# Two feed-forward tiles per half moved from plain products to the seven-product scheme, in a two-layer encoder step

## What is computed

```python
def _swiglu(x, w_gate, w_up, w_down):
    return (jax.nn.silu(x @ w_gate) * (x @ w_up)) @ w_down
# in _layer, twice:
h = h + 0.5 * _rmsnorm(_swiglu(_rmsnorm(h, g[0]), f1g, f1u, f1d), g[1])
```

## Time and profile before

| | |
|---|---|
| runs | 2678.25, 2678.82, 2679.03 us; median 2678.82 us |
| profiled execution | 2683.69 us by its own clock, of which 2681.9 us are the span of the trace |
| granted TensorE clock, mean | 0.992 of 2.4 GHz |
| instructions in the trace | 56799 |
| matmuls | 17818 |

### The profile page before, as it was taken

One profiled execution on the slowest core, in us unless ns is written; L12 is line 12 of the kernel. 1 busy time (PEld: TensorE's weight loads), 2 busy tenths in 40 slices (PEclk: granted clock), 3 DMA queues, 4 the chain that ended last, 5 costly groups with the idle time before them and its releaser, 6 DMA issues.

```text
span 2681.9 us, 56799 instructions
## 1 busy us (share of the span) xinstructions
PE 2631.2 (98%) x17818; PEld 2590.4 (97%) x17818; DVE 1721.9 (64%) x2619; ACT 1083.6 (40%) x1953; POOL 908.1 (34%) x731
## 2 busy tenths in 40 slices
PE   8999999999999999999999999999999999999998
PEld 7999999989999999999999999998999999999997
DVE  6888823575444788882388885265644448888625
ACT  5444513333333544451354444142333335454413
POOL 4665302240001566530256651142200025666112
PEclk9999999999999999999999999999999999999999
DMA  4223223222222222322223232232122222322222
GB/s 122 80 78 93 76 85 83 69 65 69 72 79 67 77 79 78 91 77 85 79 71 89 78 88 85 72 90 72 50 76 78 76 76 59 91 78 86 87 72 93
DMA packets 435462, 212.91 MB, mean 79 GB/s; under 512 B 45016, under 2 KB 433594, under 8 KB 435258
## 3 DMA queue, kind: packets, MB, share of 16 engines
q1 hardware_dynamic: 431652, 207.27, 26.9%
q10 hardware_dynamic: 3638, 3.51, 0.4%
HBM read 207.21 MB, written 5.29 MB: 79 GB/s over the span
## 4 chain that ended last, share of the span: by engine, by line
PE 92%; DVE 4%; issue 2%; ACT 1%; DVEq 0%; POOL 0%; DMA 0%; ACTq 0%; SPq 0%; POOLq 0%
PE ps L741 11%; PE ps L742 11%; PE ps L743 11%; PE ps L649 9%; PE ps L651 9%; PE ps L650 9%; PE ps L832 7%; PE ps L833 7%; PE ps L834 7%; PE ps L677 5%; PE ps L729 4%; DVE h L1685 1%; DVE x_r L1667 1%; PE ps L880 1%; PE ps L902 1%
## 5 line engine op out<-in xcount | busy, mean ns | idle before, releaser
L2315 POOL TENSOR_TENSOR w_lo<-raw,w_hi 128x512 fp32r<-128x512 f32 x288 | 429.0, 1500 | 357.8 <-ACT w_hi L1102 356.1
L741 PE MATMUL ps<-x_r,w_hi 128*128 128x320 f32 x1728 | 534.6, 309 | 3.1 <-ACT u L1102 2.8
L743 PE MATMUL ps<-x_r,w_lo 128*128 128x320 f32 x1728 | 533.9, 309 | 0.0
L1649 DVE TENSOR_TENSOR w_lo<-raw,w_hi 128x1024 fp32r<-128x1024 f32 (+1 forms) x240 | 297.6, 1243 | 355.5 <-ACT w_hi L1110 355.3
L2266 POOL TENSOR_TENSOR acc_y<-acc_y,sq 128x320 f32<-128x320 f32 x96 | 94.4, 984 | 1105.7 <-ACT sq L1120 1104.0
L742 PE MATMUL ps<-x_r,w_hi 128*128 128x320 f32 x1440 | 444.9, 309 | 0.0
L1110 ACT ACTIVATE w_hi<-raw 128x1024 fp32r<-128x1024 f32 (+1 forms) x248 | 253.5, 1027 | 468.0 <-PE ps L834 301.2
L832 PE MATMUL ps<-mid_hi,w_hi 128*128 128x320 f32 x1408 | 437.6, 311 | 0.0
L833 PE MATMUL ps<-mid_lo,w_hi 128*128 128x320 f32 x1408 | 436.1, 310 | 0.0
L834 PE MATMUL ps<-mid_hi,w_lo 128*128 128x320 f32 x1408 | 436.0, 310 | 0.0
L649 PE MATMUL ps<-x_r,w_hi 128*128 128x320 f32 x1088 | 346.8, 319 | 4.3 <-DVE w_lo L1649 4.3
(11 more groups left out here) (216 smaller groups left out, 5069.2 us busy)
## 6 DMA issues: line engine op xcount, KB each, us to landing
raw<-in_ffn_w_gate_dram SPq DMA_DIRECT2D x360, 128.0 KB, 2.3
raw<-in_ffn_w_up_dram SPq DMA_DIRECT2D x360, 128.0 KB, 2.3
raw<-in_ffn_w_down_dram SPq DMA_DIRECT2D x348, 128.0 KB, 2.2
raw<-in_w_in_dram SPq DMA_DIRECT2D x304, 128.0 KB, 2.3
raw<-in_w_branch_dram SPq DMA_DIRECT2D x64, 128.0 KB, 2.6
raw<-in_w_out_dram SPq DMA_DIRECT2D x64, 128.0 KB, 2.2
raw<-in_ffn_w_down_dram SPq DMA_DIRECT2D x68, 64.0 KB, 1.9
rows<-in_x_prompt_dram SPq DMA_DIRECT2D x4, 512.0 KB, 5.4
```

The lines of the kernel that those rows point to most:

```text
L741: pe.matmul(bank(b), wh, lhs(0, k), start=begin and k == 0, stop=False, skip_group_check=True)
L743: mm = pe.matmul(bank(b), wl, lhs(0, k), start=False, stop=k == QK - 1, skip_group_check=True)
L1649: dve.tensor_tensor(w_cols(1, hi_slot, 0, nk), raw_cols(raw_slot, 0, nk), f32(w_cols(0, hi_slot, 0, nk)), ALU.subtract).then_inc(w_split, 1)
L2315: pool.tensor_tensor(w_cols(1, slot, k0, k0 + QK), src, f32(w_cols(0, slot, k0, k0 + QK)), ALU.subtract).then_inc(ws_lo, 1)
```

## The change

`PLAIN` goes from 4 to 2: `extra_four` and all that serves it (its four loads, high and low parts, eight scalings) go away, `first_four` stays, and each FFN has 20 units instead of 18. The hand-written lists of ACT and DVE for the head are reordered; POOL's list and PE's order inside the units stay as they are, but P1 of unit 0 now stands right behind `first_four`. The four silus that remain come after `next_high(0, 0)` on ACT, and their four `head_mid` products stand together ahead of DVE's loop. S4 (`sum4`) and the low parts of S3 change places on DVE.

```diff
-PLAIN = 4
+PLAIN = 2
-HEAD_T, HEAD_LOADS, RESTAGED = 4, 2, 2
+HEAD_T, HEAD_LOADS, RESTAGED = 4, 1, 2
...
@@ SP
-                for s in range(HEAD_T):
-                    load(s, columns(w_ffn[n][s % 2], l, 0, KD, (2 + s // 2) * P, s), (w_split, w0 + s + 1))
                 for u in range(2):
-                    unit(u, PLAIN // 2, [(w_split, w0 + HEAD_T + 2 * u + 1), (w_split, w0 + HEAD_T + 2 * u + 2)])
+                    unit(u, PLAIN // 2, [(w_split, w0 + 2 * u + 1), (w_split, w0 + 2 * u + 2)])
...
@@ PE
+                pe.wait_ge(evac, g + 4 + 5)
                 p1(0, 0)
-                pe.wait_ge(evac, g + 4 + 12)
+                pe.wait_ge(inv_x_made, 2 * (3 * l + 2 * n) + 2)
                 p2(0, 0)
...
                 first_four(hi0(l, n), split0(l, n), g, seam, Y_SQUARES_MIX if n else Y_SQUARES)
-                extra_four(split0(l, n), g, seam)
                 strassen(n, l, g)
...
@@ ACT
                 roots(BX[1], sm - 1, 3, False)
-                extra_high(0)
-                head_silu(0, 0)
-                extra_high(1)
+                w0_high(0, HEAD_LOADS, (group_done, g + 5))
                 keep_inv_x(1, sm - 1)
-                extra_high(2)
-                head_silu(1, 0)
-                extra_high(3)
-                for i in range(8):
+                for i in range(4):
                     sum_hi(i)
-                head_silu(0, 1)
-                head_silu(1, 1)
-                w0_high(0, HEAD_LOADS, (group_done, g + 10))
-                head_silu(2, 0)
-                head_silu(2, 1)
-                t_high(0, "T2", 0, (group_done, g + 12))
-                t_high(0, "T1", 0, (group_done, g + 12))
+                t_high(0, "T2", 0, (group_done, g + 6))
+                t_high(0, "T1", 0, (group_done, g + 6))
+                for i in range(4, 8):
+                    sum_hi(i)
+                t_high(0, "T3", 0, (group_done, g + 7))
+                t_high(0, "T4", 0, (group_done, g + 7))
+                snap(1, 0, 0)
                 for k in range(QK):
-                    sum_hi(2 * QK + k)
-                t_high(0, "T3", 0, (group_done, g + 14))
-                t_high(0, "T4", 0, (group_done, g + 14))
-                head_silu(3, 0)
-                head_silu(3, 1)
+                    s3_high(k)
                 b22_high(0, HEAD_LOADS, (group_done, g + PLAIN_G))
                 b22_high(1, HEAD_LOADS, None)
-                for k in range(QK):
-                    s3_high(k)
-                snap(1, 0, 0)
                 w0_high(1, HEAD_LOADS, (prod, p0 + 2))
                 snap(2, 0, 0)
                 snap(3, 0, 0)
+                for k in range(QK):
+                    sum_hi(2 * QK + k)
                 next_high(0, 0)
+                for hf in range(2):
+                    for f in range(PLAIN):
+                        head_silu(f, hf)
                 silu(gate_scaled, gs0 + 1, PLAIN, 0)
                 end_unit(0, 0, 0, 1)
...
@@ DVE
                 inverse(sm - 1, 3)
-                extra_low(0)
-                for k in range(QK):
+                for k in range(2):
                     sums12(k)
+                t_first(0, 0, HEAD_LOADS)
+                for k in range(2, QK):
+                    sums12(k)
+                w0_low(0, 0)
+                t_second(0, 0)
                 second_half(sm - 1)
                 scale_first(1)
-                extra_low(1)
-                scale_extra(0)
-                extra_low(2)
-                w0_low(0, 0)
-                t_first(0, 0, HEAD_LOADS)
-                scale_extra(1)
-                t_second(0, 0)
-                extra_low(3)
+                for k in range(QK):
+                    s3_low(k)
                 for k in range(QK):
                     sum4(k)
-                scale_extra(2)
-                scale_extra(3)
-                for k in range(QK):
-                    s3_low(k)
                 w0_low(1, 1)
...
                 dve.wait_ge(silu_done, sl0 + HEAD_MIDS)
                 dve.wait_ge(evac, g + 4 + PLAIN_G)
                 alone(dve)
+                for j in range(HEAD_MIDS):
+                    head_mid(j)
                 with dve.Fori(0, UNITS // 2 - 1) as i:
-                    head_mid(i)
                     body(1, i * 2 + 1, i)
```

More of the change, by code:

```diff
@@ L205, in trunk_kernel @@
         FIRST_BANKS = ((0, 1, 2, 3), (0, 4, 6, 7))
-        EXTRA_BANKS = (1, 2, 3, 5, 4, 6, 7, 1)
         BANK_A, BANK_D, BANK_E = (0, 1), (2, 3), 5
@@ L714, in first_four @@
                 low_of_x(1)
[L716 to L731, removed]
             def product(what, u, lhs, b, begin, ready=None):
@@ L1178, in free @@
                     return (group_done, v) if kind == "group" else (chunk_done, ch0 + v)
-                def extra_high(s):
-                    stage(raw_full(s, l, n, 1), s, KD, (group_done, g + 4 + s + 1), s)
                 def head_silu(f, hf):
-                    act.wait_ge(evac, g + (4 * hf + 2 * f if f < 2 else 8 + 4 * (f - 2) + hf) + 5)
+                    act.wait_ge(evac, g + 4 * hf + 2 * f + 5)
                     act.activation(tile(mid, f, hf), tile(mid, f, hf), ACT.Silu).then_inc(silu_done, 1)
@@ L1725, in scale_first @@
                         scale((plain_gate, plain_up)[s % 2](2 * (s // 2) + hf), FIRST_BANKS[hf][s], hf, g + 4 * hf + s)
[L1727 to L1732, removed]
                 def head_mid(j):
@@ L1888, in ffn @@
                 last_quarters(0, 0, 0)
-                assert HEAD_MIDS == UNITS // 2 - 1
                 dve.wait_ge(silu_done, sl0 + HEAD_MIDS)
```

## The result

The changed kernel takes **2729.99 us** (median of 4 runs, 2729.23 to 2732.1), the kernel before 2678.53 us beside it (4 runs, 2676.95 to 2679.03): ratio 1.0195 (1.018 to 1.021), 51.5 us more; 2733 us were forecast. The profiled execution took 2730.72 us with a span of 2728.9 us, 47.0 us more than the span before. That of before lay 4.9 us above its median, that of after only 0.7 us; in what follows the traces account for 47.0 us, 11.75 per FFN. The other 4.5 us may be the clock, which isn't shown: the profiled execution of before has a mean granted clock of 0.992, as has one more execution of that kernel (2683.62 us), and eight others (2676.34 to 2678.96 us) have 0.993 to 0.995. The two traces themselves differ in this too: after the wait of the earlier trace rows the clock is lower in all four FFNs of the trace of before, and in two of that of after.

What follows compares the result with a forecast made beforehand. PE, busy 98% of the span, was taken to bound the kernel. Per FFN 6.8 + 1.8 + 5.3 + 1.8 + 1.3 - 3.5 = 13.5 us more, times four 54 us on 2678.8: 2733 us, range 2705 to 2758.

Steps and rivals of the forecast that it cites:

- What goes away: On PE, 24 fewer matmuls per FFN at 0.147 us save 3.5 us; DMAs were put at nothing.
- P1 of unit 0: After `first_four`, PE waits 6.8 us for DVE's first scaling of half 1; bounds 4.3 and 8.7.
- P1 of unit 1: PE waits 5.3 us for DVE's `w0_low`, behind S3's low parts and `sum4`; bounds none to 6.9.
- the eight DVE instructions: S3's low parts and `sum4` all meet POOL: five at 1.55, three at 1.0, 10.8 us together.
- P6 of units 0 and 1: PE waits 1.8 us before each, for POOL's low part of T2 and for ACT's `snap` 1 of unit 1.
- The clock: Lower granted clock after a wait costs PE 1.3 us; one such loss per head (0 to 5.2).
- POOL costs DVE little: Rival: in the new order they miss each other; waits of 7 us per head, 2692 to 2705 us; chance 0.08.
- The clock falls at every wait: Rival: all four waits of a head cost 1.3 us, 3.9 more per head, 2749 us; chance 0.13.
- DVE becomes the bound after the head: Rival: units 1 to 3 wait for `c22_out` 1 to 3 us more, 2737 to 2745 us; chance 0.09.
- Faster: Rival: unit 0's preparation still fits under `first_four`; without any wait 2664.7 us; chance 0.04.
- The rule on DVE beside POOL: Whole-instruction lock makes a pair 1.78 us, 3 us more per head, 2745 us; prediction stayed with the rows' 1.55.
- The rule on the clock: Skill page's kernel fell to the lower clock at each wait because its matmuls between waits were short.

Runs made afterwards that it cites:

- x1: Changed kernel plus 192 idle matmuls between `first_four` and P1 of unit 0, new list order kept; 2797.34 us, ratio 1.0442.
- x6: Changed kernel plus 192 idle matmuls after `first_four`, with ACT's and DVE's lists back in the old order; 2781.7 us, ratio 1.0383.
- x4: Changed kernel plus idle matmuls inside the two waits, 42 before P1 of unit 0 and 26 before P1 of unit 1; 2728.94 us, ratio 1.0187.
- x3: Changed kernel with POOL writing zeros for the low parts of S1, S2, S4 and unit 0's five weight parts; 2707.13 us, ratio 1.0106.
- x2: Changed kernel with `w0_low` and the first scaling on DVE after one k's sums, other sums behind the weight differences; 2732.38 us, ratio 1.02.
- x5: Changed kernel plus 96 idle matmuls between `first_four` and P1 of unit 0; 2745.51 us, ratio 1.0248.
- x8: Changed kernel with `w0_low` of unit 1 moved ahead of the four `sum4` in DVE's list; 2730.89 us, ratio 1.0194.
- x7: Kernel before, with DVE's sum for P3 in the last unit moved ahead of a staging step and six low parts; 2669.98 us, ratio 0.9967.

## Why the prediction was right, and where its terms were not

The total was 3 us off (2733 against 2729.99, in a range of 2705 to 2758), for the reason given: the preparation of unit 0 lost its cover. By spans it foresaw 54 us and 47.0 came; that the medians agree better is luck, since the profiled execution of before lay further above its median than that of after. Its steps:

- **What goes away.** 96 matmuls, as counted, with a price per matmul that x1 and x6 bear out (192 idle ones fill 28.2 us per FFN). No wait for a load turned up.
- **P1 of unit 0: right.** 6.8 us were predicted and 27.0/4 = 6.8 measured. Inside, two errors cancel in part: both first weight differences ran alone, 0.68 each, not one at 1.29; the four sums beside POOL took 4.3, not 4.0, and the first scaling came at 62.55 + 0.42, 0.7 earlier than worked out. PE started 0.3 behind it, and `first_four` was through 0.2 before the 56.9 of the prediction, which makes up for most of that: the place and the releaser were reasoned, the equal tenths are luck.
- **P1 of unit 1: right in place and releaser, too large.** 5.3 predicted, 17.2/4 = 4.3 measured. The failed term is the eight DVE instructions: 8.7 us in place of 10.8, against which S3 came 0.9 us later than worked out (67.87 for 67.0). Their price beside POOL was right (1.5 for 1.55 beside a weight part, 1.1 for 1.0 beside a low part of S4); but the prediction let all eight meet POOL, and three of them met it hardly or not at all.
- **P6 of units 0 and 1: not there in after.** Two times 1.8 us were predicted. T2's low part came at about 68.2 (69.0 predicted), while PE came to P6 only at 68.70, because the lower clock had stretched P1 and P2. For P6 of unit 1 `snap` was done at 87.2 (88.5 predicted), and PE came there at 88.2 (86.7 predicted). The step that failed is that both terms were worked out with PE at full clock. x4, with PE at full clock, shows both waits, 1.7 and 1.1, released as predicted by POOL's `w_lo` and by `snap`.
- **The clock: too small.** One loss of 1.3 us per head was taken. In the first head PE made 15 matmuls in 67.38 - 63.29 = 4.09 us where 15 x 0.147 = 2.2 would do, and 22 in 5.96 where 3.2 would do: 1.9 + 2.7 = 4.6 us. So after each wait the clock's loss took the place of the wait before P6, where the prediction added the two. That 4.6 lies so near to the 1.8 + 1.8 + 1.3 = 4.9 that were put down for both is luck: x4 shows waits of 2.8 there, not of 3.6.
- **Sum of the first head:** 6.8 + 4.3 + 4.6 - 3.5 = 12.2 us. The other three heads lose less to the lower clock, 3.9, 4.1 and 3.5 us; with the mean of 4.0 the terms make 11.6, with 11.75 per FFN in the spans. The agreement is partly luck: the lower clock in the last unit, 1.3 us in the earlier trace rows, is missing after the change in two FFNs of four, some 0.65 per FFN less, and about 0.8 per FFN is left that no row here accounts for.

**The rivals.** *POOL costs DVE little* is refuted by DVE's rows (1.03 to 1.17 for 0.54), and x3 shows what it would have been worth: 2707 us, near the 2692 to 2705 given for it. *The clock falls at every wait* holds in the trace for both waits that were there, but its price does not: x4 removes the falls and saves 1 us, not the 16 that PE's lost time in the four heads comes to. *DVE becomes the bound after the head* did not happen, and the last stretch above agree on an unbroken PE. *Faster* was excluded by 6.8 us before P1 alone; x2 took that wait away by another order of DVE's list, and it stood one product further.

**The rule on DVE beside POOL.** Four DVE instructions for S3 and S4 and four weight parts of POOL, alone 0.48 (x3) and 1.30, took 1.5 us a pair, and a sum and a low part, alone 0.54 and 0.86, took 1.09. The Trainium skill, page "SBUF — State Buffer", section "SBUF: two separate sides", with its lock for a whole instruction would make 1.78 and 1.40 of them. The trace doesn't agree with that part of the rule: the two engines went nearly one after the other, with some 0.3 us of each pair side by side. The same section limits the conflict of a DVE instruction with two SBUF inputs to POOL's instructions that read SBUF, and there the trace agrees: in x3 the sum takes 0.55 beside a fill.

**The rule on the clock.** After 6.62 and after 4.30 us without work the granted clock was 0.50, with 60 matmuls between the two waits. The Trainium skill, page "TensorE: Matmul & The Clock Gate", section "HAM oscillation — how this bites in real kernels", describes this pattern, and the trace agrees; its advice to keep PE warm brought nothing here (x4), since PE wasn't what the head waited for.

What stays open: why x5 gives 1.1 us per FFN less back than the matmuls that it leaves out. It isn't the heads: from P1 of unit 0 to the 301st matmul of the units x1 and x5 take the same 49.4 to 49.9 us, head by head. The mean clock of x5 is 0.990 against 0.994 in x1, and no run shows whether that is the cause.

## What to carry to other kernels

Work that looks redundant on the bounding engine can be the cover under which the others prepare its next stage: before taking it away, add up, list by list, when the first operand of that stage would be there, with the durations that the engines have *beside each other*. If the sum says several us, reordering may only move the wait from one product to the next (x2, x8), and keeping the clock up need not shorten it (x4). A small wait that the trace names already, with one list that causes it, was worth more here than the larger change: 8.3 us faster by moving one sum (x7).

## What the hardware showed that I had not expected

- A fill on POOL (0.36 us for 128 x 320) doesn't slow DVE at all (0.55 us for the sum beside it), where a subtraction on POOL doubles it (1.03 to 1.17). POOL's being busy is not by itself what costs DVE time.
- A lower clock need not cost the kernel what it costs PE. In after it takes 3.5 to 4.6 us of PE's time in each head, and without it (x4) the heads are only 0.1 to 0.8 us shorter and the time is the same within 1 us.
- A wait of the same length doesn't always bring the lower clock: after the 2.4 us of the earlier trace rows it came in four FFNs of four in the trace of before and in two of four in that of after.
